# Loading the second quarter of x ahead of K's weights in a hybrid encoder layer

## The reference

```
h = rmsnorm(x, g_mix_pre)
q_a, k_a, v_a, q_r, k_r, v_r, g_r, gate_a, gate_r = split_in(h @ w_in)
...
x = x + rmsnorm(merged @ w_out, g_mix_post)
h = rmsnorm(x, g_ffn_pre)
f = (jax.nn.silu(h @ w_ffn_gate) * (h @ w_ffn_up)) @ w_ffn_down
x = x + rmsnorm(f, g_ffn_post)
x = x + (p @ w_ple_proj) * jax.nn.sigmoid(x @ w_ple_gate)
```

## Time and profile before

| what | value |
| --- | --- |
| median of 3 runs | 981.73 us (981.54 to 982.08) |
| the profiled execution, its own time | 981.92 us |
| span of its trace | 980.1 us |
| PE (TensorE matmul) busy | 972.4 us, 99% |
| PEld (weight load) busy | 953.5 us, 97% |
| DVE (VectorE) busy | 632.6 us, 65% |
| ACT (ScalarE) busy | 397.3 us, 41% |
| POOL (GpSimd) busy | 85.9 us, 9% |

### The profile page before, as it was taken

One profiled execution on the slowest core, in us unless ns is written; L12 is line 12 of the kernel. 1 busy time (PEld: TensorE's weight loads), 2 busy tenths in 40 slices (PEclk: granted clock), 3 DMA queues, 4 the chain that ended last, 5 costly groups with the idle time before them and its releaser, 6 DMA issues.

```text
span 980.1 us, 18690 instructions
## 1 busy us (share of the span) xinstructions
PE 972.4 (99%) x7286; PEld 953.5 (97%) x7286; DVE 632.6 (65%) x1247; ACT 397.3 (41%) x698; POOL 85.9 (9%) x140
## 2 busy tenths in 40 slices
PE   8999999999999999999999999999999999999998
PEld 7999999999999999999999999999999999999997
DVE  5554676757665633435458899625997469975772
ACT  5333533434343522222455555424453234544352
POOL 2123212112100000010003000000000000030000
PEclk9999999999999999999999999999999999999999
DMA  8434221222222232245603523521334213366221
GB/s 215 136 112 130 83 67 55 66 76 64 63 69 66 76 91 83 76 126 171 198 2 116 207 86 88 150 66 45 108 102 124 76 45 109 100 192 201 87 55 44
DMA packets 166229, 98.68 MB, mean 101 GB/s; under 512 B 14672, under 2 KB 162544, under 8 KB 165888
## 3 DMA queue, kind: packets, MB, share of 16 engines
q1 hardware_dynamic: 159920, 79.19, 28.6%
q0 software_dynamic: 4336, 16.67, 4.8%
q10 hardware_dynamic: 1888, 1.64, 0.5%
HBM read 86.79 MB, written 10.75 MB: 100 GB/s over the span
## 4 chain that ended last, share of the span: by engine, by line
PE 98%; DMA 1%; DVE 0%; SPq 0%; ACT 0%; issue 0%; DVEq 0%; ACTq 0%
PE acc L693 37%; PE acc L970 11%; PE acc L971 11%; PE acc L972 11%; PE small L970 6%; PE small L971 6%; PE small L972 6%; PE small L839 1%; PE small L885 1%; PE small L856 1%; PE small L889 1%; PE small L848 1%; PE small L887 1%; PE acc L801 1%; DMA x_row<-in_x_sample 1%; PE small L870 1%
## 5 line engine op out<-in xcount | busy, mean ns | idle before, releaser
L693 PE MATMUL acc<-xh,whi 128*128 128x288 f32 x720 | 158.8, 301 | 0.1
L693 PE MATMUL acc<-xh,wlo 128*128 128x288 f32 x720 | 153.4, 294 | 0.0
L693 PE MATMUL acc<-xl,whi 128*128 128x288 f32 x720 | 153.4, 294 | 0.0
L1159 ACT ACTIVATE whi<-raw 128x1024 fp32r<-128x1024 f32 (+1 forms) x61 | 61.1, 1002 | 197.7 <-PE acc L693 196.1
L693 PEld LDWEIGHTS acc<-xh,whi 128*128 128x128 f32 x720 | 113.9, 188 | 5.8 <-issue 4.7
L693 PEld LDWEIGHTS acc<-xh,wlo 128*128 128x128 f32 x720 | 115.0, 188 | 0.0
L693 PEld LDWEIGHTS acc<-xl,whi 128*128 128x128 f32 x720 | 115.0, 188 | 0.0
L1991 DVE TENSOR_TENSOR wlo<-raw,whi 128x512 fp32r<-128x512 f32 (+2 forms) x93 | 81.0, 872 | 50.9 <-ACT whi L1376 35.3
L970 PE MATMUL acc<-yh,whi 128*128 128x288 f32 x360 | 107.0, 297 | 0.0
L972 PE MATMUL acc<-yh,wlo 128*128 128x288 f32 x360 | 106.1, 295 | 0.0
L1664 DVE TENSOR_TENSOR wlo<-raw,whi 128x1024 fp32r<-128x1024 f32 (+1 forms) x63 | 73.0, 1159 | 44.7 <-ACT whi L1159 43.8
(11 more groups left out here) (333 smaller groups left out, 2396.1 us busy)
## 6 DMA issues: line engine op xcount, KB each, us to landing
raw<-in_w_in SPq DMA_DIRECT2D x92, 256.0 KB, 3.2
raw<-in_w_ffn_gate SPq DMA_DIRECT2D x44, 256.0 KB, 3.4
raw<-in_w_ffn_up SPq DMA_DIRECT2D x44, 256.0 KB, 4.2
raw<-in_w_ffn_down SPq DMA_DIRECT2D x32, 256.0 KB, 3.8
res<-x_scratch POOLq DMA_DIRECT2D x16, 288.0 KB, 4.5
raw<-in_w_branch_ret SPq DMA_DIRECT2D x16, 256.0 KB, 3.0
raw<-in_w_out SPq DMA_DIRECT2D x16, 256.0 KB, 4.7
raw<-in_w_ffn_down SPq DMA_DIRECT2D x16, 192.0 KB, 3.9
```

What stands on the lines that cost most here:

```text
L693: ins = nc.tensor.matmul(acc[:, a, hf, 0:HALF], w[:, s, at:at + P], x(k)[:, hf * HALF:(hf + 1) * HALF], start=first and n == 0 and m == 0, ...
L1159: nc.scalar.activation(whi[:, s, 0:n], raw[:, s, 0:n], ACT.Copy).then_inc(hi_ready, 1)
```

## The change

`x_quarter(1)` moves up past the load of K's weights. The issue order becomes: x quarter 0, x quarter 1, K's weights, x quarter 2, V's weights, x quarter 3. Nothing else is changed.

```diff
@@ -602,8 +602,8 @@
                 sp.dma_start(x_row[0:DEC, RT - 1, cols], x_s[0][:, cols]).then_inc(x_in[q], 16)
 
             x_quarter(0)
+            x_quarter(1)
             columns(unit(U_KV), wi, C_KA)
-            x_quarter(1)
             x_quarter(2)
             columns(unit(U_KV + 1), wi, C_VA)
             x_quarter(3)
```

## The result

The changed kernel took 985.63 us (median of 6, 984.73 to 986.05) against 981.83 us before (median of 6, 981.47 to 982.08): a ratio of 1.0037, 95% interval 1.0026 to 1.0047. It is slower by 3.8 us, where +1.5 and no more than 984.2 had been forecast. The profiled execution of the changed kernel took 984.95 us. One of the later executions of the changed kernel took 1353.55 us at a mean granted clock of 0.655 and is left out of all that follows.

A forecast was written before the change was run, and what follows sets the result against it. TensorE was taken to wait for nothing after about 17 us, so its early start bounds the kernel. K's later weights add 1.53 us and the clock nothing: from the median of 981.73 to 983.3 us, range 982.2 to 984.2.

The forecast's parts named there:

- some 0.6 us of slack: K's weights could land 0.59 us later before the transposes of tile 2 wait, 0.66 before K's first matmul does.
- x's arrival was only just the last of three waits: Before tile 2's work, x's second quarter came last, 0.59 us behind the copy to `x_t`; K's low part was the third.
- the landing of K's second transfer: On SyncE's queue K's weights would land at 10.1 us in place of 8.02, bounds 9.4 and 11.0.
- its two workings: Two estimates of K's landing: 10.22 by equal bytes moved on the queue, 9.98 by adding intervals; the middle was taken.
- the copy as what the transposes wait for: ScalarE's copy of tile 0 to `x_t`, ending at 11.75, would release tile 2's transposes at 11.79 us.
- K's first matmul at 12.58: On TensorE K's first matmul would start at 12.58 against 11.05 us, +1.53.
- the stretch of 6 us to V that shifts whole: From tile 2's transposes each step releases the next, so V's first matmul moves from 17.02 to 18.55 us.
- the delay goes to the end with nothing to absorb it: TensorE shows no waits from about 17 us to the last tile, so an early delay reaches the end one for one.
- The term itself: The cost of K's later weights on the path to K's first matmul: +1.53 us.
- the one on TensorE's clock: TensorE's pause before tile 2's transposes grows from 1.33 to 2.9 us; the clock's cost, bounded by 0 and 1.3, taken as nothing.
- this rival: The clock falls in the longer pause before tile 2's transposes: 1.53 + 1.3 = +2.8, 984.6 us; chance 0.12.
- the five cases: The forecast of 983.3 us and four rivals: clock falls 984.6, K lands still later 984.1, K follows its issue 982.5, x's wait goes 981.1.

The follow-up runs named there:

- twice the dose: Kernel before with x's quarters 1 and 2 both ahead of K's weights and 22 products of ones in TensorE's pause: 985.45 us.
- fill14: Changed kernel with 14 in place of 5 products of ones behind tile 1's transposes, so TensorE works through the wait: 983.22 us.
- after_again: Changed kernel run again with no edit: 984.69 us against 982.28 for the kernel before beside it.
- before_no_ones: Kernel before, loads untouched, without the 5 products of ones behind tile 1's transposes: 984.18 us.
- sample_first: Kernel before with 9 in place of 5 products of ones and only the sample's 64 KB of x's second quarter ahead of K's weights: 982.08 us.
- copy_first6: Changed kernel with ScalarE's copy of tile 0 ahead of K's high-part split and 6 products of ones behind tile 2's transposes: 983.43 us.
- half_split: Kernel before, loads untouched, K's weights split in two halves and K's tile 0 worked off ahead of tile 2's transposes: 981.80 us against 982.28.

## Why the prediction was wrong

**What held.** The reading that K's weights had some 0.6 us of slack (0.5 by the runs) and that x's arrival was only just the last of three waits; the landing of K's second transfer at 10.05 (10.1 forecast), though one of its two workings was right by luck (it put x's second quarter 2.0 us behind the first and K 2.35 behind that, and they came some 2.7 and 1.6 behind, with the second quarter in at 8.4 and not 7.6); the copy as what the transposes wait for; K's first matmul at 12.58 against 12.57; the stretch of 6 us to V that shifts whole (5.97 before, 5.98 in the trace of the changed kernel without a fall, 5.97 at twice the dose); that the delay goes to the end with nothing to absorb it. `fill14`, which has the changed order and no fall, took 983.22 us; the forecast said 983.3. The term itself came out a little smaller on the chip of that run, 1.0 to 1.1 us against 982.2 for the kernel before without a fall. K's weights were split 0.2 us earlier in that trace; the rest is not explained beyond the scatter of the kernel before.

**The step that failed** is the one on TensorE's clock: "I take nothing, since the nearest row (1.33) lost nothing, and keep the other as a rival", with a chance of 0.12. The pause came out as foreseen (2.73 us against 2.9), and behind it the clock fell in 12 of 16 executions of the changed kernel. One trace of the kernel before was taken as proof that a pause of 1.33 us is safe, and that proof was carried over to one twice as long. It is not even safe there: 16 of 82 executions of the kernel before fell. A single profile shows one outcome of something that differs from one execution to the next, and the nearest row was one draw. The range, 982.2 to 984.2, left this rival outside on purpose.

**Its size.** The rival was priced at 1.3 us, half of the 2.6 us that the clock took to rise at the start. In the trace it was 1.53, and by medians 1.7 among the ten executions of `after_again` and 1.9 over all: 985.2 with and 983.3 without the fall for the changed kernel, 984.1 and 982.2 for the kernel before. The price held roughly, and the rival's time of 984.6 was the nearest of the five cases to the 985.63 measured. The Trainium skill's warning in "TensorE: Matmul & The Clock Gate", "Why this matters for your kernels", that an idle stretch between bursts of matmuls brings the clock back to half, is for stretches longer than the 2.73 us measured here, a condition that the prediction did not give. The trace shows the same fall, 0.50 from 13 to 16.3 us, behind this shorter pause, and that of `before_no_ones` shows it behind 2.16 us. Here the measurement decides: a shorter pause than the Trainium skill warns of there can cost the clock.

**What stays open:** what beside the length of the pause decides whether the clock falls (it fell behind 2.16 us and not behind 2.19, in two kernels with different work ahead of the pause), and the long executions at a full clock: two near 985 in `sample_first`, 984.1 and 985.4 in `copy_first6`, and one of 984.2 of the kernel before.

## What to carry to other kernels

Before a load is moved ahead of another, look at how much later the second-last arrival is than the last: here the wait that the profile named was worth 0.6 us at most, and the load that paid for it had 0.5 us of slack and landed 2.0 later. Where a change lengthens a pause of TensorE, price the fall of its clock as likely, not as a footnote, and look at the mean granted clock of many executions, as one profile shows one outcome. A pause that can't be shortened is cheaply filled with products that nothing reads, or better with work that is there: in `half_split` half of K's weights were enough to start on.

## What the runs showed of the hardware beyond that

The rise of the clock at the start differs between executions of the same instructions too. The 20 matmuls of ones took 3.96 us in the trace of before and 4.63 in that of the changed kernel:

```profile
1.11 3.96 PE L757 MATMUL acc<-ones 128*128 128x128 f32 x20 [1.11 <-DVE rowsum L1675]
```

```profile
1.11 4.63 PE L757 MATMUL acc<-ones 128*128 128x128 f32 x20 [1.11 <-DVE rowsum L1675]
```

The granted clock is shown as 1.00 in both stretches, though single matmuls took 421 ns there and 275 later. That is a factor of 1.5, and the transposes within the stretch at 0.50 show much the same, 1.26 us for five in place of 0.80. So at the start of an execution it is the durations that point to the lower level; the clock column does not show it.
